# First weight panel, decay groups and squares moved within the opening of a hybrid decoder layer

## The chip, the cores and the metric

One core of a Trainium2 chip runs the whole kernel. The metric is the device time of one execution in microseconds (us). TensorE is PE in the profile (PEld its weight loads), VectorE is DVE, ScalarE is ACT, GpSimd is POOL, and SyncE (SP) issues the transfers.

## The reference, cut to what matters

One inference step of a decoder layer for two request groups that share weights: 1024 prompt tokens and 8 sequences of 4 sample tokens, 1056 tokens of 1024 features. The part that the change touches is the start:

```python
h = rmsnorm(x, norm_mix)                 # x * rsqrt(mean(x*x) + eps) * gain
proj = h @ w_in                          # 1024 -> 3592 columns: q, k, v, a, b, z and the short convolution
log_a = -exp(a_log) * softplus(proj[..., OFF_A:OFF_B] + dt_bias)   # decay of the delta rule, 4 columns
beta = sigmoid(proj[..., OFF_B:OFF_Z])                             # 4 columns
```

Behind it come the convolution and SiLU of q, k and v, the chunked gated delta rule, the short convolution mixer, the output projection, an MLP of 1024 to 4096 to 1024, an embedding gate, and a last norm. All are in float32.

## The kernel before, in words

Every float32 product is made of three products in a faster format: a value is split into a high part (rounded) and a low part (value minus high part), and high by high, low by high and high by low are summed. ACT makes the high parts, DVE and POOL the low ones. Activations lie as features by tokens (`act_hi`, `act_lo`), and the norm's factor per token is not applied to x but to the products, so that the products may start before the sums of squares are known.

The opening works on nine tiles of x, `x_tok[0]` to `x_tok[8]`: eight of 128 tokens and one of the 32 sample tokens. Each tile has two halves of four blocks of 128 features, numbered i = 2t and 2t+1. For a half, PE turns four blocks into one of four PSUM banks `bk[i % 4]` (line 753); DVE multiplies the bank by the norm's gain into one of four SBUF buffers `ring[i % 4]` (line 1575, "weighing"); ACT copies the buffer into `act_hi` (the high part; the helper's line is 1150); and the low part, buffer minus high part, is made by DVE for the even half (line 1578) and by POOL for the odd half (line 2127). PE may reuse a bank once it is weighed (`xw_made`), and DVE may reuse a ring buffer once its low part exists (`xlo_even`, `xlo_odd`). The ring and the banks hold two tiles.

The first weight panel, number 0, holds the eight columns for the decay and beta. ACT splits it (`split_w(0, 0)`, all 1024 columns of elements), and DVE makes its small low part of 64 columns (line 1538, same helper `split_w`). Its products with the tokens are three "decay groups", `ab_group(0)` to `ab_group(2)`, each of 16 matmuls over a third of the tokens (352): `ab_group(0)` needs tiles 0 to 2, `ab_group(1)` needs tiles 0 to 5. DVE copies each result out (`ab_rows`, line 1564) over the place of `x_tok[0]` and the first bytes of `x_tok[1]`, so the first of these waits for the first two sums of squares. Panel 1 is the first of the q columns; `first_group(n)` are its 24 matmuls for third n.

The sums of squares of x by token (`square(t)`, on ACT, 1024 elements a row) lead to the norm's factor: a square root on ACT, a reciprocal, two diagonals `AT` and a small one `X` on DVE (lines 1586 to 1591), and then four matmuls on PE that spread the factor over the partitions (lines 777 to 779), behind `first_group(1)`.

Every engine runs its list strictly in the order written. PE has: turns of tiles 0 to 4, `ab_group(0)`, turns of 5 to 7, `ab_group(1)`, turns of 8, the turns of the old states (lines 764 and 766), `first_group(0)`, `ab_group(2)`, `first_group(1)`, the spreading matmuls, `first_group(2)`, and then the panels one after the other. ACT has: high parts of tile t, then `square(t)` for t up to 3, `split_w(0)` behind tile 2 and `split_w(1)` behind tile 5; behind tile 8 come squares 4 to 8 and the root. DVE has: for each tile its weighing and its low part, `split_w(0)` behind tile 3, `split_w(1)` behind tile 6, `ab_rows(0)` behind tile 5, `ab_rows(1)` and `ab_rows(2)` behind tile 8. SP issues the loads of x and of panel 0 first (line 538 and 526). Its load of panel 2 waits for the split of panel 0, its load of panel 3 for that of panel 1.

Of the kernel before, what the change touches and what calls it, by code (L numbers as in the profile page):

```python
# [18 lines left out]
NTT = TP // P  # L19
# [222 lines left out]
def trunk(nc, x_p, x_s, st_qkv, st_gdn, st_sc, p_p, p_s, norm_mix, w_in, w_cq, a_log, dt_bias, w_gn, w_cs,  # L242
# [19 lines left out]
    with ctx:  # L262
# [127 lines left out]
        sm = Signals(sem)  # L390
# [4 lines left out]
        def at(base, p=0, step=1):  # L395
            return base if isinstance(p, int) and p == 0 else p * step + base

        def twelfths(b, p, q):
            return at(12 * b + q, p, 24)

        def cols(n):
            return slice(n * TH, (n + 1) * TH)

        def tokens(t):
            return P if t < NTT else TS

        def heads(ap):
            return ap.rearrange("p (h t) -> p h t", h=H)

        def spread(ap, n):  # L410

            return ap[:, :, None].to_broadcast([ap.shape[0], ap.shape[1], n])
# [35 lines left out]
        def last_product(hf, g):  # L448

            return (g // 3, g % 3) if hf == 0 else (g % 4, g // 4)  # L450
# [238 lines left out]
        def _(pe):  # L689
            mm, turn = nc.tensor.matmul, nc.tensor.transpose  # L690

            def products(bank, terms):

                for i, (w, a) in enumerate(terms):
                    last = mm(pg[bank][:, 0:TH], w, a, start=i == 0, stop=i == len(terms) - 1)  # L695
                return last
# [7 lines left out]
            def panel_ready(b, p):  # L704
                pe.wait_ge(sm.w_lo_made, at(b + 1, p, 2))
# [10 lines left out]
            def ab_group(n):  # L716

                terms = [(w_hi[0][:, k, :], a[:, k, cols(n)]) for k in range(KD) for a in (act_hi, act_lo)]
                products(n, terms).then_inc(sm.ab_mm, 1)
# [24 lines left out]
            for t in range(NTT + 1):  # L744
                n = tokens(t)
                pe.wait_ge(x_loaded[t], 16)
                for hf in range(2):
                    i = 2 * t + hf
                    if i >= 4:
                        pe.wait_ge(sm.xw_made, i - 3)  # L750
                    for k in range(4):
                        f = slice((4 * hf + k) * P, (4 * hf + k + 1) * P)
                        last = turn(bk[i % 4][:, k * P:k * P + n], x_tok[t][0:n, f], ident[0:n, 0:n])
                    last.then_inc(sm.x_turned, 1)

                if t in (4, 7):
                    whole = 3 if t == 4 else 6
                    pe.wait_ge(sm.xlo_even, whole)
                    pe.wait_ge(sm.xlo_odd, whole)
                    panel_ready(0, 0)  # L760
                    ab_group((t - 4) // 3)
            pe.wait_ge(sm.states_in, 32)
            for j in range(NQ):
                turn(bk[4][:, j * 24:(j + 1) * 24], st_in[:, j * P:(j + 1) * P], ident[0:24, 0:24])
# [373 lines left out]
            for g in range(12):  # L1138
                d, n = last_product(1, g)
# [8 lines left out]
        def _(act):  # L1148
            def op(out, in_, func, **kw):
                return nc.scalar.activation(out, in_, func, **kw)  # L1150

            def split_w(b, p):

                if isinstance(p, int) and b + 2 * p == 2:
                    act.wait_ge(sm.ab_mm, 3)
                elif b >= 2:
                    act.wait_ge(sm.mm_done, twelfths(b - 1, p, 0))
                act.wait_ge(raw_in[b % 2], at(16 * (b // 2 + 1), p, 16))
                act.wait_ge(sm.consts_made, 3)
                op(w_hi[b % 2][:, :, :], w_raw[b % 2][:, :, :], ACT.Copy).then_inc(sm.w_hi_made, 1)  # L1160
# [6 lines left out]
            def square(t):  # L1167

                n = tokens(t)
                if t == 0:  # L1170
                    act.wait_ge(sm.r_tok_set, 2)
                else:
                    act.wait_ge(sm.x_squared, t)
                op(x_sqr[0:n, :], x_tok[t][0:n, :], ACT.Square, accum_out=r_tok[0:n, t:t + 1]) \
                    .then_inc(sm.x_squared, 1)

            act.wait_ge(sm.consts_made, 3)
            for t in range(NTT + 1):
                n = tokens(t)
                for hf in range(2):  # L1180
                    i = 2 * t + hf
                    act.wait_ge(sm.xw_made, i + 1)
                    op(act_hi[:, 4 * hf:4 * hf + 4, t * P:t * P + n], ring[i % 4][:, :, 0:n], ACT.Copy) \
                        .then_inc(sm.xhi_made, 1)
                if t < 4:
                    square(t)
                if t in (2, 5):
                    split_w((t - 2) // 3, 0)
            for t in range(4, NTT + 1):
                square(t)  # L1190
            act.wait_ge(sm.x_squared, NTT + 1)
            op(r_tok[:, :], r_tok[:, :], ACT.Sqrt, scale=1.0 / D, bias=eps[:, 0:1]).then_inc(sm.r_chain, 1)
# [303 lines left out]
            for hf in range(2):  # L1496
# [15 lines left out]
                for g in range(12):  # L1512
                    d, n = last_product(hf, g)
# [16 lines left out]
        def _(dve):  # L1530
            tt, ts_, stt = nc.vector.tensor_tensor, nc.vector.tensor_scalar, nc.vector.scalar_tensor_tensor

            def split_w(b, p):

                dve.wait_ge(sm.w_hi_made, at(b + 1, p, 2))
                if isinstance(p, int) and b + 2 * p == 0:

                    tt(w_hi[0][:, :, 2 * H:AB], w_raw[0][:, :, 0:2 * H], w_hi[0][:, :, 0:2 * H].bitcast(f32), SUB) \
                        .then_inc(sm.w_lo_made, 1)
                    return  # L1540
                tt(w_lo[b % 2][:, :, :], w_raw[b % 2][:, :, :], w_hi[b % 2][:, :, :].bitcast(f32), SUB) \  # L1541
                    .then_inc(sm.w_lo_made, 1)
# [16 lines left out]
            def ab_rows(n):  # L1559

                dve.wait_ge(sm.ab_mm, n + 1)
                if n == 0:
                    dve.wait_ge(sm.x_squared, 2)
                nc.vector.tensor_copy(qkv[0:AB, 0, cols(n)], pg[n][0:AB, 0:TH]).then_inc(sm.ab_kept, 1)


            dve.wait_ge(sm.gain_in, 16)
            for t in range(NTT + 1):
                n = tokens(t)
                for hf in range(2):  # L1570
                    i = 2 * t + hf
                    dve.wait_ge(sm.x_turned, i + 1)
                    if i >= 4:
                        dve.wait_ge(sm.xlo_odd if hf else sm.xlo_even, t - 1)
                    tt(ring[i % 4][:, :, 0:n], heads(bk[i % 4])[:, :, 0:n], spread(n_mix[:, 4 * hf:4 * hf + 4], n), MUL) \
                        .then_inc(sm.xw_made, 1)
                dve.wait_ge(sm.xhi_made, 2 * t + 1)
                tt(act_lo[:, 0:4, t * P:t * P + n], ring[2 * t % 4][:, :, 0:n],
                   act_hi[:, 0:4, t * P:t * P + n].bitcast(f32), SUB).then_inc(sm.xlo_even, 1)
                if t in (3, 6):  # L1580
                    split_w((t - 3) // 3, 0)
                if t in (5, 8):
                    ab_rows((t - 5) // 3)
            ab_rows(2)
            dve.wait_ge(sm.r_chain, 1)
            nc.vector.reciprocal(r_tok[:, :], r_tok[:, :]).then_inc(sm.r_chain, 1)
# [485 lines left out]
            for hf in range(2):  # L2072
# [18 lines left out]
                for g in range(12):  # L2091
                    d, n = last_product(hf, g)
# [288 lines left out]
```

## Time and profile before

| | us |
|---|---|
| median of 3 runs | 1523.75 (1523.41 to 1523.84) |
| the profiled execution | 1522.49 |
| its span | 1520.7 |
| PE busy in the span | 1479.3 |
| DVE busy | 734.0 |
| ACT busy | 474.0 |
| POOL busy | 246.6 |

The profile is of one execution. Its span runs from the first to the last recorded instruction, and its own time is 1.8 us longer than the span. A timeline row gives the start and the duration in us, the engine, the line, the operation, what it writes and reads, and in brackets how long the engine sat idle before it and what released it. A row that ends in x2 or x24 merges so many instructions. Instructions of one engine are pipelined, so a row's duration is somewhat more than its share of the engine's time.

### The profile page before, as it was taken

The numbers are of one execution on the slowest core, as the hardware profiler recorded it, in microseconds if no ns is written. First come the engines' busy times: TensorE is split into PE (matmuls) and PEld (weight loads), VectorE is DVE, ScalarE is ACT, GpSimd is POOL, SyncE is SP. The second block draws the span as 40 slices with busy tenths as digits, with TensorE's granted clock in tenths as the row PEclk, the third lists the DMA queues.
The fourth block names the chain that finished last, engine by engine and source line by source line (L and its number), as shares of the span: only waits on it lengthen the run. The fifth ranks groups of instructions, "written<-read, shape, count | busy, mean of one in ns | idle before, by whom it ended". The sixth has DMA issues, their size and how long they took to land.

```text
span 1520.7 us, 24673 instructions
## 1 busy us (share of the span) xinstructions
PE 1479.3 (97%) x9324; PEld 1449.6 (95%) x9324; DVE 734.0 (48%) x1313; ACT 474.0 (31%) x854; POOL 246.6 (16%) x306
## 2 busy tenths in 40 slices
PE   7999899899999999999999999999999999999997
PEld 6999898699999989999999999999999999998997
DVE  5676943287685553543333333333333334335525
ACT  6323343233243332533122130221203122135525
POOL 3200311143535363100000000000000000041303
PEclk9999998799999999999999999999999999999999
DMA  7112211412122344111111111111111111112102
GB/s 176 49 36 57 76 51 47 133 35 71 29 84 83 87 98 86 42 56 42 42 42 56 42 42 56 42 42 42 56 42 42 56 42 42 56 42 64 35 28 114
DMA packets 166315, 89.83 MB, mean 59 GB/s; under 512 B 50763, under 2 KB 160267, under 8 KB 166230
## 3 DMA queue, kind: packets, MB, share of 16 engines
q1 hardware_dynamic: 165222, 84.89, 20.1%
q0 software_dynamic: 1008, 3.79, 0.6%
q8 instruction: 55, 0.90, 0.3%
q14 instruction: 30, 0.25, 0.1%
HBM read 77.97 MB, written 10.69 MB: 58 GB/s over the span
## 4 chain that ended last, share of the span: by engine, by line
PE 88%; DVE 5%; issue 2%; POOL 2%; ACT 1%; DMA 0%; DVEq 0%; POOLq 0%; SPq 0%
PE pg L695 66%; PE pg L813 12%; PE bk L870 1%; DVE act_lo L1973 1%; PE bk L884 1%; PE bk L888 1%; PE bk L1021 1%; PE bk L840 1%; POOL act_lo L2296 1%; DVE cv L1621 0%; PE bk L854 0%; PE bk L933 0%; PE bk L930 0%; PE bk L938 0%; PE bk L921 0%
## 5 line engine op out<-in xcount | busy, mean ns | idle before, releaser
L695 PE MATMUL pg<-act_hi,w_hi 128*128 128x352 f32 x1344 | 436.1, 325 | 8.0 <-issue 3.6
L695 PE MATMUL pg<-act_lo,w_hi 128*128 128x352 f32 x1344 | 432.3, 322 | 0.0
L695 PE MATMUL pg<-act_hi,w_lo 128*128 128x352 f32 x1320 | 423.7, 321 | 0.0
L695 PEld LDWEIGHTS pg<-act_hi,w_hi 128*128 128x128 f32 x1344 | 253.1, 188 | 11.3 <-issue 7.3
L695 PEld LDWEIGHTS pg<-act_lo,w_hi 128*128 128x128 f32 x1344 | 253.7, 189 | 0.0
L695 PE MATMUL pg<-u_hi,w_hi 128*128 128x352 f32 x768 | 249.3, 325 | 0.0
L695 PE MATMUL pg<-u_hi,w_lo 128*128 128x352 f32 x768 | 248.9, 324 | 0.0
L695 PEld LDWEIGHTS pg<-act_hi,w_lo 128*128 128x128 f32 x1320 | 248.0, 188 | 0.0
L695 PE MATMUL pg<-u_lo,w_hi 128*128 128x352 f32 x768 | 247.8, 323 | 0.0
L1150 ACT ACTIVATE w_hi<-w_raw 128x1024 fp32r<-128x1024 f32 x111 | 117.0, 1054 | 350.4 <-PE pg L695 320.1
L2337 POOL TENSOR_TENSOR ssq<-ssq,sq 128x352 f32<-128x352 f32 x72 | 76.2, 1067 | 875.1 <-ACT sq L1150 874.4
L2034 DVE TENSOR_TENSOR xres<-xres,pg 128x352 f32 (+1 forms) x192 | 99.2, 520 | 201.0 <-PE pg L695 201.0
L1541 DVE TENSOR_TENSOR w_lo<-w_raw,w_hi 128x1024 fp32r<-128x1024 f32 x110 | 139.3, 1266 | 65.4 <-ACT w_hi L1150 65.2
L813 PE MATMUL pg<-act_hi,w_hi 128*128 128x352 f32 x480 | 162.7, 339 | 2.0 <-DVE pre L1598 1.6
L813 PE MATMUL pg<-act_hi,w_lo 128*128 128x352 f32 x480 | 162.3, 338 | 0.0
L813 PE MATMUL pg<-act_lo,w_hi 128*128 128x352 f32 x480 | 160.0, 333 | 0.0
L695 PEld LDWEIGHTS pg<-u_hi,w_hi 128*128 128x128 f32 x768 | 145.0, 189 | 0.0
L695 PEld LDWEIGHTS pg<-u_lo,w_hi 128*128 128x128 f32 x768 | 144.5, 188 | 0.0
L695 PEld LDWEIGHTS pg<-u_hi,w_lo 128*128 128x128 f32 x768 | 143.9, 187 | 0.0
L1150 ACT ACTIVATE sq<-tm 128x352 f32<-128x352 f32 x96 | 47.8, 498 | 231.8 <-DVE tm L2020 231.8
L2024 DVE TENSOR_TENSOR u_lo<-sq,u_hi 128x352 f32 x96 | 50.4, 525 | 129.1 <-ACT u_hi L1150 129.1
L813 PEld LDWEIGHTS pg<-act_hi,w_hi 128*128 128x128 f32 x480 | 93.2, 194 | 7.9 <-issue 5.8
(331 smaller groups left out, 1655.5 us busy)
## 6 DMA issues: line engine op xcount, KB each, us to landing
w_raw<-in_w_up SPq DMA_DIRECT2D x32, 512.0 KB, 4.0
w_raw<-in_w_down SPq DMA_DIRECT2D x32, 512.0 KB, 3.3
w_raw<-in_w_in SPq DMA_DIRECT2D x29, 512.0 KB, 4.4
x_tok<-in_x_prompt SPq DMA_DIRECT2D x8, 512.0 KB, 7.4
w_raw<-in_w_out SPq DMA_DIRECT2D x8, 512.0 KB, 4.1
x_col<-in_x_prompt SPq DMA_DIRECT2D x32, 128.0 KB, 2.6
w_raw<-in_w_ple_gate SPq DMA_DIRECT2D x8, 512.0 KB, 3.9
out<-y_tok SPq DMA_DIRECT2D x8, 512.0 KB, 2.9
```

Source lines behind the costliest of these rows:

```text
L695: last = mm(pg[bank][:, 0:TH], w, a, start=i == 0, stop=i == len(terms) - 1)
L813: last = mm(pg[n][:, 0:TH], w, (act_hi, act_lo, act_hi)[r][:, k, cols(n)], start=k == 0 and r == 0, stop=k == KD - 1 and r == 2)
L840: last = mm(bk[4][:, c:c + 8], S_in[:, h, i, :], F0[:, c:c + 8], start=True, stop=True)
L870: per_head(lambda h, v: mm(A[x][:, v], LY[x][:, h, :], X[x][:, h, :], start=True, stop=True)) \
L884: last = per_head(lambda h, v: mm(A[x][:, v], XT[s][x][:, h, :], LY[x][:, h, :], start=True, stop=True))
L888: last = per_head(lambda h, v: mm(bank[:, v], LY[x][:, h, :], XT[s][x][:, h, :], start=True, stop=True))
L1021: mm(bk[c % 4][:, :], F0[0:TS, c // 2 * P:(c // 2 + 1) * P], by_seq[c % 4][0:TS, :, :], start=True, stop=True).then_inc(sm.q_pe, 1)
L1150: return nc.scalar.activation(out, in_, func, **kw)
L1541: tt(w_lo[b % 2][:, :, :], w_raw[b % 2][:, :, :], w_hi[b % 2][:, :, :].bitcast(f32), SUB) \
L2024: tt(rows(u_lo[c % 2][:, k, cols(n)]), sq[g % 2][:, :], rows(u_hi[c % 2][:, k, cols(n)]).bitcast(f32), SUB).then_inc(sm.u_lo_made, 1)
L2034: tt(x_t, x_t, pg[g % 3][:, 0:TH], ADD).then_inc(sm.evacuated, 2)
L2337: tt(ssq[:, cols(n)], ssq[:, cols(n)], sq[g % 2][:, :], ADD).then_inc(sm.ssq_added, 1)
```

## The change

On PE the first two decay groups go one tile earlier: `ab_group(0)` behind tile 3 and `ab_group(1)` behind tile 6. On ACT, `split_w(0)` goes behind tile 1 (from 2), `split_w(1)` stays behind tile 5, and the squares follow three tiles behind the high parts: `square(t - 3)` from tile 3 on, and squares 5 to 8 after the loop. On DVE the weighing of tile t+1 stands ahead of the low part of tile t, `split_w(0)` goes behind the low part of tile 1 (from 3), `split_w(1)` behind that of tile 5 (from 6), and `ab_rows(0)` and `ab_rows(1)` behind tiles 4 and 7 (from 5 and 8).

```diff
@@ PE
-                if t in (4, 7):
-                    whole = 3 if t == 4 else 6
-                    pe.wait_ge(sm.xlo_even, whole)
-                    pe.wait_ge(sm.xlo_odd, whole)
+                if t in (3, 6):
+                    pe.wait_ge(sm.xlo_even, t)
+                    pe.wait_ge(sm.xlo_odd, t)
                     panel_ready(0, 0)
-                    ab_group((t - 4) // 3)
+                    ab_group((t - 3) // 3)
@@ ACT
-                if t < 4:
-                    square(t)
-                if t in (2, 5):
-                    split_w((t - 2) // 3, 0)
-            for t in range(4, NTT + 1):
+                if t in (1, 5):
+                    split_w((t - 1) // 4, 0)
+                if 3 <= t < NTT:
+                    square(t - 3)
+            for t in range(NTT - 3, NTT + 1):
                 square(t)
@@ DVE
-            for t in range(NTT + 1):
+            def x_weighed(t):
...
+            x_weighed(0)
+            for t in range(NTT + 1):
+                n = tokens(t)
+                if t < NTT:
+                    x_weighed(t + 1)
                 dve.wait_ge(sm.xhi_made, 2 * t + 1)
                 tt(act_lo[:, 0:4, t * P:t * P + n], ring[2 * t % 4][:, :, 0:n],
                    act_hi[:, 0:4, t * P:t * P + n].bitcast(f32), SUB).then_inc(sm.xlo_even, 1)
-                if t in (3, 6):
-                    split_w((t - 3) // 3, 0)
-                if t in (5, 8):
-                    ab_rows((t - 5) // 3)
+                if t in (1, 5):
+                    split_w((t - 1) // 4, 0)
+                if t in (4, 7):
+                    ab_rows((t - 4) // 3)
```

## Rows read from the trace of the kernel before

**Rows 1.** The page: the chain that ended last, by engine.
```profile
PE 88%; DVE 5%; issue 2%; POOL 2%; ACT 1%; DMA 0%; DVEq 0%; POOLq 0%; SPq 0%
```

**Rows 2.** Window: length; PE, PEld, DVE, ACT, POOL busy; granted clock; DMA.
```profile
44.00:130.00 86.00, 86.00 (x547) 85.84 (x547) 59.59 (x98) 23.61 (x40) 7.01 (x35) 1.00 0.13 36
```

**Rows 3.** Timeline of PE where the norm's factor comes in.
```profile
40.88 0.32 PE L695 MATMUL pg<-act_hi,w_lo 128*128 128x352 f32 x1
41.57 1.12 PE L777 MATMUL bk<-AT,ones 128*128 128x512 f32 x2 [0.37 <-DVE X L1591]
```

**Rows 4.** Timeline of ACT: high parts, squares, table load, root.
```profile
23.71 1.23 ACT L1150 ACTIVATE act_hi<-PT 128x512 fp32r<-128x512 f32 x2 [3.76 <-DVE PT L1575]
...
31.26 1.05 ACT L1150 ACTIVATE x_sqr<-x_tok 128x1024 f32<-128x1024 f32 x1
...
37.15 1.28 ACT L1150 ACT_TABLE_LOAD   x1
38.44 0.30 ACT L1150 ACTIVATE r_tok<-r_tok,eps 128x9 f32<-128x9 f32 x1
```

**Rows 5.** Timeline of PE, 7 to 27 us: turns and decay groups.
```profile
7.20 1.97 PE L753 MATMUL bk<-ident,x_tok 128*128 128x128 f32 x8 [0.46 <-DMA x_tok<-in_x_prompt]
...
10.27 5.38 PE L753 MATMUL bk<-ident,x_tok 128*128 128x128 f32 x24 [1.10 <-DMA x_tok<-in_x_prompt]
...
18.23 0.40 PE L695 MATMUL pg<-act_hi,w_hi 128*128 128x352 f32 x1 [2.58 <-DVE w_hi L1538]
...
18.63 0.32 PE L695 MATMUL pg<-act_hi,w_hi 128*128 128x352 f32 x1
...
20.72 0.49 PE L695 MATMUL pg<-act_hi,w_hi 128*128 128x352 f32 x1
...
21.89 3.34 PE L753 MATMUL bk<-ident,x_tok 128*128 128x128 f32 x24
...
26.39 0.40 PE L695 MATMUL pg<-act_hi,w_hi 128*128 128x352 f32 x1 [1.16 <-issue]
```

**Rows 6.** Timeline of DVE: low part, small split, weighing, copy of a decay group.
```profile
12.90 0.69 DVE L1578 TENSOR_TENSOR act_lo<-XT,act_hi 128x512 fp32r<-128x512 f32 x1
...
16.78 1.31 DVE L1538 TENSOR_TENSOR w_hi<-w_raw,w_hi 128x64 fp32r<-128x64 f32 x1
...
24.99 0.51 DVE L1564 COPY qkv<-pg 16x352 f32<-16x352 f32 x1
25.42 1.27 DVE L1575 TENSOR_TENSOR XT<-bk,n_mix 128x512 f32<-128x512 f32 x2
```

**Rows 7.** Timeline of POOL: the odd low parts of tiles 2 and 3.
```profile
13.71 1.29 POOL L2127 TENSOR_TENSOR act_lo<-XT,act_hi 128x512 fp32r<-128x512 f32 x1 [1.04 <-ACT act_hi L1150]
16.73 1.27 POOL L2127 TENSOR_TENSOR act_lo<-PT,act_hi 128x512 fp32r<-128x512 f32 x1 [1.74 <-ACT act_hi L1150]
```

**Rows 8.** The load of panel 0, issued at 2.37 us: KB, us to landing.
```profile
w_raw<-in_w_in SPq DMA_DIRECT2D x1, 512.0 KB, 6.6
```

**Rows 9.** Windows of the turns alone: length, PE busy, granted clock, DMA.
```profile
11.00:15.00 4.00, 4.00 (x20) 1.00 1.03 410
22.00:23.00 1.00, 1.00 (x6) 0.50 1.02 7
23.25:24.75 1.50, 1.50 (x17) 1.00 0.88 199
```

**Rows 10.** Windows of PE: length, busy, granted clock, DMA.
```profile
20.00:21.50 1.50, 1.50 (x7) 0.50 0.68 5
157.00:163.00 6.00, 5.93 (x22) 0.50 0.00 0
298.50:303.00 4.50, 0.00 (x0) 0.99 0.99 282
304.00:309.50 5.50, 5.50 (x22) 0.50 0.21 55
265.50:282.00 16.50, 16.50 (x33) 0.50 0.50 160
```

## The prediction, made before the changed kernel was run

> **What bounds the kernel now.** I read the page first, then busy time by stretch, then the start of the chain of waits, and last the timelines of each engine up to 45 us. The chain that ended last is 88% PE [rows 1], and from 44 to 130 us PE is busy without a gap [rows 2], with what follows hanging on its products. So whatever the opening gains or loses arrives behind it one for one. The opening ends at 41.57 us, where PE starts the matmuls that spread the norm's factor. It waited 0.37 us for DVE's `X`, its last product before ends at about 41.04 (the row at 40.88 is the last of its pace of 0.16), so PE's own list is 0.5 us behind being the bound there [rows 3]. Both must come earlier for a gain; one of them later is enough for a loss.
>
> Two chains, then. ACT's: squares 4 to 8 start at 31.26, follow each other every 1.18 us (five to 37.15), the table load takes 1.28, the root starts at 38.44 [rows 4], and `X` is out at about 41.5, 3.1 later. PE's: turns of tiles 2 to 4 from 10.27 for 5.38; idle for 2.6 until the small split of panel 0; `ab_group(0)` from 18.23; turns of 5 to 7 from 21.89; 1.1 idle; `ab_group(1)` from 26.39 [rows 5]; tile 8, turns of the states and 64 matmuls in a row (24, 16 and 24, 10.3 us).
>
> **The change part by part.** *Panel 0 on DVE and ACT.* Before, the small split ran 16.78 to 18.09, 1.31 for 64 columns [rows 6]. It ended right behind POOL's low part of tile 3, 16.73 to 18.00 [rows 7]: DVE's operations on two SBUF operands and POOL's exclude each other in this trace, while the weighings, which read PSUM, pass. Now ACT splits the panel behind tile 1. The weighing of tile 1 can't start before its turns (7.20 to 9.17, [rows 5]), so its high parts end at about 10.5, the split (1.05 in the page's group) at 11.5; the panel's load, issued at 2.37, lands 6.6 later, at 9.0 [rows 8]. DVE's low part of tile 1 still follows the weighing of tile 2, at 12.90 [rows 6], as tile 2's turns begin at 10.27 when it lands, and the small split goes at 13.5, ahead of POOL's low part of tile 2 at 13.71.
>
> *Start of `ab_group(0)`.* What is late next is the even low part of tile 2. It stands behind the weighing of tile 3: 13.65 to 14.9 (a pair is 1.27, [rows 6]). It then meets POOL's low part of tile 2, 13.71 to 15.00 [rows 7], and runs 15.0 to 15.7. `ab_group(0)` starts at 15.8 instead of 18.23: 2.45 us earlier. Without that exclusion it would be 15.7.
>
> *PE's clock.* The row says 1.00 for the early turns, but 24 turns in 5.38 us are 0.224 each. Where the row says 0.50, they go at that pace (6 met in 1 us), and at a true 1.00 some 0.12 each (17 met in 1.5 us) [rows 5, 9]. So PE starts at the lower level (1.2 GHz) and the profile's row only shows 1.00 for lack of an earlier record. It was at 2.4 GHz by 18.2 (matmuls 0.16 apart), fell at 19.7 behind the idle 2.6 us, and `ab_group(0)` ended at the low pace, 0.29 apart [rows 5, 10]. The Trainium skill says the same of the start ("TensorE: Matmul & The Clock Gate", section "What's actually happening"): the default is the throttled state, and activity releases it; it also warns of idle gaps. By the page's row alone (2.4 GHz from the start) `ab_group(0)` would take 2.6 us and the change would come out as my second case below; by the skill's it starts slow.
> Now PE has done 3.6 us of turns (10.27 to 13.86) and idled 1.9 when `ab_group(0)` starts. The rises in this trace stand behind 5.4 us of turns, 6 us of work (157 to 163) and 5.5 us (304 to 309.5) [rows 5, 10]. Bounds: 16 matmuls at 0.16 are 2.6, at 0.29 are 4.7. I take the level as low for 13 and high for the last 3, 4.3 us, near the low end: the end at 20.1. Behind it come turns of tiles 4 to 6 at 0.12, to 23.1 (before: 5 to 7, to 25.2).
>
> *`ab_group(1)`.* It needs the even low part of tile 5. Before, DVE made low parts while PE was in `ab_group(0)`; now the low part of tile 3 stands behind the weighing of tile 4, whose turns stand behind `ab_group(0)`. From 20.1: first half turned and seen, 0.7; weighing 4, 1.3; low 3, 0.6; weighing 5, 1.25; low 4, 0.6, and 0.3 more against POOL's odd low part of tile 4; `ab_rows(0)`, 0.45; weighing 6, 1.25; low 5, 0.7; PE's start, 0.1 (prices from [rows 6], back to back somewhat under a row's duration). That is 7.2 in all with rounding: 27.1 to 27.3, against 26.39: **+0.75**. DVE becomes the bound here, and PE idles 4.0 us (23.1 to 27.1) where it idled 1.1.
>
> *Clock again.* In 298.5 to 303 the clock fell inside an idle of 5.5 us and PE then worked 5.5 us at 0.50 [rows 10]; at 18 it fell behind one of 2.6. I take it that it falls in the idle of 4.0. Bounds for `ab_group(1)`: nothing, if it doesn't, and 16 x 0.133 = 2.1 if all its matmuls are slow, with slow turns behind. I take 10 slow ones: **+1.3**.
>
> *The tile that moved.* Between `ab_group(1)` and `first_group(0)` PE now turns tile 7 too, 8 x 0.12 = **+0.95**, and a gap of 0.1 before tile 8 goes: **-0.1**. So `first_group(0)` starts at 33.6 instead of 30.7, +2.9, and PE is through `first_group(1)` at 43.95 instead of 41.04. There it no longer waits for `X`: **-0.5**. Sum **+2.4**.
>
> *Squares.* One of five leaves the end of ACT's list, -1.18 in ACT's chain, but tile 8's high part is late: weighing 7 at 31.6, low 6, weighing 8 at 33.5, high part to 34.6, four squares to 39.3, table, root at 40.6, `X` at 43.7. The saving is hidden behind PE (43.95). Square 1, for which `ab_rows(0)` waits, ends at 23.9, before 24.7. The squares 0, 2 and 3 fill idle time of ACT. `split_w(1)` on DVE goes at about 27 with `ab_group(1)` beside it; SP's load of panel 3 moves with it, from 28.6, and its panel is wanted tens of us later. Nothing else is issued more or less often.
>
> The profiled execution had 1522.49 with a span of 1520.7; the sum makes it 1524.9. The runs' median is 1.26 above the profiled one, so **1526.15**, 0.16% above 1523.75. A measurement of this kernel can tell about 0.2% (3 us) from nothing, so in that sense this is no change.
>
> **Rivals.** *Second case: the clock is high by 16 us and stays.* For it: the early rows say 1.00, and tile 3's turns before it are much like those that did release it. Against it: the idle of 4 us is longer than the one that cost the clock. `ab_group(0)` ends at 18.4, DVE's 7.0 puts `ab_group(1)` at 25.4, `first_group(0)` at 30.7, as before; ACT's root is 0.3 earlier and the waiting 0.37 shrinks: -0.35, 1523.4. If the clock is high for the first group and falls before the second, 25.4 start, 9 slow matmuls and slow turns put `first_group(0)` at 32.2: +0.9, 1524.7.
> *Third case, slower: the clock comes back late.* The place is `ab_group(1)` and the turns behind it. If the clock rises only some 6 us into work, as from 157 to 163 and from 304 on [rows 10], all 16 matmuls are slow (+0.8 more) and tile 7's turns (+0.8). The start of `first_group(0)` is then 35.2, the sum +4.0, 1527.8. It decides from an idle of PE long enough for the clock to fall before `ab_group(1)` starts. For it: the two rows. Against: the rise at 23.0 came 4.8 us after work began at 18.2.
> *Fourth case: later falls of the clock meet other work.* There are stretches at 0.50 in which PE is the chain, 265.5 to 282 and 304 to 309.5 [rows 10]. Their work at twice the pace would be 8 and 3 us. If the clock's changes don't move with the work, a shift of 1 to 3 us lengthens or shortens them by a few us. Runs 0.4 us apart speak for a steady pattern that a shift could break. Taken with cases one or two this gives 1520 to 1529.
> *The change doesn't do what it says:* `ab_group(0)` could start no earlier if panel 0 were late; the load's landing at 9.0 excludes it.
>
> **How the numbers follow.** Forecast case 0.45, second case (with its half-way form) 0.27, third 0.13, fourth beyond 3 us either way 0.15, rather more of it fast. The range takes the first three with 1 us around the ends and part of the fourth: 1521.2 to 1528.6; the likeliest case's own is 1525.0 to 1527.3. Slower by over 3 us (above 1526.8): a fifth of the forecast case's upper edge (0.09), the third (0.12) and a part of the fourth: 0.25. Faster by over 3 us (below 1520.7): 0.11, nearly all by the fourth, as no term of the opening gives more than 1 us. Within: 0.64.
>
> **What would show it.** `ab_group(0)` at 15.8 and its matmuls 0.29 apart at first; DVE idle from 15.7 to about 20.8; `ab_group(1)` at 27.1 behind DVE's low part of tile 5, with PE idle 4 us before; `first_group(0)` at 33.6; PE at line 777 at 44.0 with no wait for `X`. The forecast is wrong if line 777 starts before 41.6, if the clock stays high through both groups, or if the traces' difference at 130 us is not that at 44 us.

## The result, and the profile after

The changed kernel takes 1527.53 us in the median of 22 runs (1524.04 to 1529.71), the kernel before 1524.32 in 22 runs beside it (1521.59 to 1526.02): ratio 1.0020, interval 1.0014 to 1.0027, some 3 us slower. A second set (`after_again`, below) gave 1.0013 (1.0004 to 1.0022). The forecast was +2.4 us, 1526.15. Here and below a time is the median of the runs; the ratio is estimated from all of them, with its 95% interval in brackets, and needn't be that of the two medians.

The profiled execution took 1526.67 with a span of 1524.9. The first view is the timeline of PE (start, duration, engine, line, what it writes and reads, in brackets the idle time before and what ended it). It answers to [rows 5] and [rows 3]. A matmul of a group starts 0.16 us behind the one before at the higher clock and 0.29 behind it at the lower.

```profile
10.50 3.45 PE L753 MATMUL bk<-ident,x_tok 128*128 128x128 f32 x16 [1.08 <-DMA x_tok<-in_x_prompt]
...
16.75 0.32 PE L695 MATMUL pg<-act_lo,w_hi 128*128 128x352 f32 x1
...
17.41 0.49 PE L695 MATMUL pg<-act_hi,w_hi 128*128 128x352 f32 x1
...
19.76 3.10 PE L753 MATMUL bk<-ident,x_tok 128*128 128x128 f32 x24
26.87 0.43 PE L695 MATMUL pg<-act_hi,w_hi 128*128 128x352 f32 x1 [4.01 <-DVE act_lo L1584]
...
43.80 0.32 PE L695 MATMUL pg<-act_hi,w_lo 128*128 128x352 f32 x1
44.15 1.12 PE L776 MATMUL bk<-AT,ones 128*128 128x512 f32 x2
```

The second is the chain of waits over the same stretch (start, duration, engine, what it writes, line). It shows when each group began and how long it took, up to the end of its last matmul, which is somewhat behind the start of what follows.

```profile
15.85 4.12 PE pg L695 x16
...
26.87 4.39 PE pg L695 x16
...
33.72 10.40 PE pg L695 x64
```

The reader is to see that the first decay group starts 2.4 us sooner than before (15.85 for 18.23) and the second half a microsecond later (26.87 for 26.39), behind 4.0 us in which PE has nothing to do. From then on everything is late: the first spreading matmul (line 776) starts at 44.15 instead of 41.57, +2.58. In the first group the quick matmuls come first (16.75) and the slow ones behind (17.41).

Third, DVE's timeline (columns as above). Between the low part at 15.11 and the weighing at 20.72 it stands idle for 4.9 us, and then the low parts of tiles 3 (21.92), 4 and 5 stand in a row, each behind the weighing of a later tile. The last row is the making of `X`.

```profile
13.72 0.22 DVE L1537 TENSOR_TENSOR w_hi<-w_raw,w_hi 128x64 fp32r<-128x64 f32 x1
...
15.11 0.68 DVE L1584 TENSOR_TENSOR act_lo<-XT,act_hi 128x512 fp32r<-128x512 f32 x1
20.72 1.29 DVE L1575 TENSOR_TENSOR XT<-bk,n_mix 128x512 f32<-128x512 f32 x2 [4.93 <-PE bk L753]
21.92 0.68 DVE L1584 TENSOR_TENSOR act_lo<-PT,act_hi 128x512 fp32r<-128x512 f32 x1
22.71 1.29 DVE L1575 TENSOR_TENSOR PT<-bk,n_mix 128x512 f32<-128x512 f32 x2
23.91 0.68 DVE L1584 TENSOR_TENSOR act_lo<-XT,act_hi 128x512 fp32r<-128x512 f32 x1
...
24.95 1.27 DVE L1575 TENSOR_TENSOR XT<-bk,n_mix 128x512 f32<-128x512 f32 x2
26.14 0.67 DVE L1584 TENSOR_TENSOR act_lo<-PT,act_hi 128x512 fp32r<-128x512 f32 x1
...
42.83 1.26 DVE L1597 TENSOR_SCALAR X<-ident,r_tok 32x32 f32<-32x32 f32 x1
```

Fourth, windows of PE (length, busy, granted clock, DMA share, GB/s). The clock is at the lower level (0.50 is 1.2 GHz) for most of both groups. In both it was still at the higher level when the group started (the matmuls up to 16.91 are 0.16 us apart, and the row at 27.00 has 1.00) and fell at 17.0 and at 27.3. From 44 to 130 us PE is busy all the time, as in [rows 2], so most of the 2.6 us is carried on: the matmuls of line 813 (812 in the changed kernel) begin at 129.64 before and at 132.01 now, +2.4.

```profile
17.00:18.00 1.00, 1.00 (x6) 0.50 1.15 186
...
27.00:27.20 0.20, 0.20 (x2) 1.00 0.57 4
27.50:30.50 3.00, 3.00 (x12) 0.50 0.65 24
...
44.00:130.00 86.00, 85.97 (x541) 1.00 0.14 38
```

The spans differ by 4.2 us, and the remaining 1.6 us comes later: the row at 304.00 in [rows 10]'s stretch, where PE resumes behind a wait of 5.5 us, answers to one at 308.09, +4.1. How much of that is the change is asked below.

### The profile page after: what moved, and what is told of

Same layout as the page of the kernel before. It is cut to its first block, busy times and chain, and to the rows that moved or that the text cites. A ratio compares the mean times of both kernels' runs of the same rounds, so it can differ in the third digit from the quotient of the medians.

```text
span 1524.9 us, 24673 instructions
## 1 busy us (share of the span) xinstructions
PE 1480.6 (97%) x9324; PEld 1451.0 (95%) x9324; DVE 733.2 (48%) x1313; ACT 473.9 (31%) x854; POOL 245.8 (16%) x306
## 4 chain that ended last, share of the span: by engine, by line
PE 89%; DVE 5%; issue 2%; POOL 2%; ACT 1%; DMA 0%; SPq 0%; DVEq 0%; POOLq 0%
PE pg L695 67%; PE pg L812 12%; PE bk L869 1%; DVE act_lo L1979 1%; PE bk L883 1%; PE bk L887 1%; PE bk L1020 1%; PE bk L839 1%; POOL act_lo L2302 1%; PE bk L1130 1%; DMA x_tok<-in_x_prompt 0%; DVE cv L1627 0%; PE bk L853 0%; PE bk L932 0%; PE bk L929 0%
```

## The experiments

The theory is that of the prediction: the first decay group stands ahead of tile 4's turns, so DVE has nothing to do during it and pays its low parts afterwards; PE waits for them, the clock falls in or just behind the wait, and a tile's turns are left for behind the second group. The rivals: weighing a tile ahead is the fault; both groups' places count alike; the squares set the end; or it is the clock's chance. All ratios are to the kernel before, run on the same chip.

**Both groups back** (`groups_back`).

```diff
-                if t in (3, 6):
+                if t in (4, 7):
...
-                if t in (4, 7):
-                    ab_rows((t - 4) // 3)
+                if t in (5, 8):
+                    ab_rows((t - 5) // 3)
```

> The changed kernel with only its decay groups back behind tiles 4 and 7 (their copies on DVE behind tiles 5 and 8). Theory: the loss comes from PE standing behind a decay group while DVE's low part of an older tile stands behind a weighing that PE hasn't turned yet, and from the clock that falls in that idle. With tile 4 turned before the first group, DVE has work during it: first group at 15.9 us, second at about 23.2 (26.87 in the changed kernel), first_group(0) at 27.6, first spreading matmul at about 38 (44.15), so about 6 us faster than the changed kernel and 3.5 us faster than the kernel before. Rival, that weighing a tile ahead is what costs: second group still at 26 or later and the spreading matmul above 42, no gain over the kernel before.

Measured: 1520.48 against 1524.35, 0.9974 (0.9965 to 0.9984), 3.9 us faster than before. The timeline and the chain of this kernel:

```profile
15.89 0.43 PE L695 MATMUL pg<-act_hi,w_hi 128*128 128x352 f32 x1 [0.24 <-DVE act_lo L1584]
...
23.13 0.43 PE L695 MATMUL pg<-act_hi,w_hi 128*128 128x352 f32 x1 [1.79 <-DVE act_lo L1584]
...
37.80 1.02 PE L776 MATMUL bk<-AT,ones 128*128 128x512 f32 x2
```

```profile
15.89 2.84 PE pg L695 x16
...
23.13 2.84 PE pg L695 x16
```

All of the forecast starts are met within 0.2 us, and both groups take 2.84 us instead of 4.12 and 4.39. Everything else of the change, weighing ahead included, is still in this kernel. So the loss lies in where the groups stand.

**DVE's order back** (`low_first`).

```diff
-            x_weighed(0)
             for t in range(NTT + 1):
                 n = tokens(t)
-                if t < NTT:
-                    x_weighed(t + 1)
+                x_weighed(t)
```

> The changed kernel with only DVE's order back (weighing of a tile directly ahead of its own low part). Theory: the low part of tile 3 leaves the chain to the second group and that of tile 4 is done sooner, but PE still turns tile 4 behind the first group: second group at about 26.0 us (26.87), first_group(0) at 32.9, spreading matmul at 43.4, about 0.7 us faster than the changed kernel and 1.9 slower than before. Rival, that weighing ahead is the whole loss: spreading matmul at 41.6 or earlier, no slower than the kernel before.

Measured: 1528.84 (6 runs) against 1524.35, 1.0029 (1.0017 to 1.0041). The second group started at 26.08 for the 26.0 forecast, but that is luck: the forecast went by a slow first group, and here the first was fast (2.81 us). Where it was fast with the new order (`after_again`), the second started at 25.40, so the old order makes it 0.7 us later, not 0.9 sooner (one profile each). The clock was low through all of the second group and the spreading matmul came at 44.15, not at 43.4:

```profile
26.08 5.03 PE pg L695 x16
...
44.15 1.12 PE bk L776 x2
```

The forecast time was missed by 2.6 us (4.5 slower than before for 1.9 forecast). What follows is that the order isn't the fault: with the old order the changed kernel is no better.

**The early split alone** (`split_alone`), in the kernel before.

```diff
+                if t == 1:
+                    split_w(0, 0)
                 if t < 4:
                     square(t)
-                if t in (2, 5):
-                    split_w((t - 2) // 3, 0)
+                if t == 5:
+                    split_w(1, 0)
...
-                if t in (3, 6):
-                    split_w((t - 3) // 3, 0)
+                if t in (2, 6):
+                    split_w((t - 2) // 4, 0)
```

> The kernel before with only the split of panel 0 early (ACT behind the high parts of tile 1, DVE behind the low part of tile 2). Theory: the first group starts at about 15.7 us (18.23) right behind the turns of tile 4, PE doesn't idle, the clock stays at the higher level, the second group starts at about 22.4, first_group(0) at 26.5, spreading matmul at about 37: some 4 us faster than before. Rival, that an early split gains nothing since ACT's squares set the spreading matmul: it stays at 41.5, same time as before.

Measured: 1521.96 against 1524.35, 0.9981 (0.9973 to 0.9990), 2.4 us faster. The spreading matmul came at 38.31, later than the 37 forecast, and PE waited for `X`:

```profile
38.31 1.12 PE L777 MATMUL bk<-AT,ones 128*128 128x512 f32 x2 [0.37 <-DVE X L1593]
```

This part of the change is worth 3.3 us in the opening. The rival (that it stays at 41.5) falls, since tile 8 and with it the last five squares also come sooner (the first of them at 28.01 instead of 31.26).

**Work for PE in the wait** (`filler`), in the changed kernel.

```diff
+                if t == 6:
+                    for r in range(22):
+                        mm(pg[2][:, 0:TH], w_hi[0][:, r % KD, :], act_hi[:, r % KD, cols(0)], start=True, stop=True)
```

> The changed kernel with 22 more matmuls of 352 columns on PE between the turns of tile 6 and the second decay group, written to a bank that nothing reads before it is written anew; they fill about 3.5 of the 4 us of idle time. Theory: the clock stays at the higher level in the second group, which takes 2.6 instead of 4.4 us; the spreading matmul comes at about 42.5 (44.15), 1.6 us faster than the changed kernel, about 1 slower than before. Rival, that the clock isn't part of the loss: second group as long as before, or the filler delays it, 0 to 0.5 us slower than the changed kernel.

Measured: 1524.34 against 1524.35, 1.0000 (0.9992 to 1.0009): with 22 needless matmuls the changed kernel is as fast as the kernel before. Its chain:

```profile
15.41 5.06 PE pg L695 x16
...
27.51 2.83 PE pg L695 x16
...
43.25 1.13 PE bk L779 x2
```

The second group took 2.83 us instead of 4.39. The first was slow throughout in this execution (5.06 for 4.12), which is why the spreading matmul came at 43.25 and not at 42.5. That the clock is part of the loss is shown by this kernel; the runs put that part at 2 to 3 us, the trace at 1.5, and the difference between these is not settled.

**One group back at a time** (`first_back`, `second_back`), in the changed kernel.

```diff
-                if t in (3, 6):
+                if t in (4, 6):
...
-                if t in (4, 7):
-                    ab_rows((t - 4) // 3)
+                if t in (5, 7):
+                    ab_rows((t - 5) // 2)
```

> The changed kernel with only its first decay group back behind tile 4 (the second stays behind tile 6; DVE copies behind tiles 5 and 7). Theory: the first group's place is what costs, since tile 4's weighing then runs beside it: first group at 15.9 us, second at 23.1, tile 7 is turned behind it, first_group(0) at 28.5, spreading matmul at about 38.8: 5 us faster than the changed kernel, 1 us slower than with both groups back. Rival, that both places count alike: second group at 25 or later, spreading matmul at 41.

```diff
-                if t in (3, 6):
+                if t in (3, 7):
...
-                if t in (4, 7):
-                    ab_rows((t - 4) // 3)
+                if t in (4, 8):
+                    ab_rows((t - 4) // 4)
```

> The changed kernel with only its second decay group back behind tile 7 (the first stays behind tile 3; copies behind tiles 4 and 8). Theory: the second group still starts at 26.9 us, as DVE's low part of tile 5 is what it waits for; tile 7's turns move into the idle time, so first_group(0) comes 0.95 sooner, at 32.8, spreading matmul at 43.2, 1 us faster than the changed kernel and 1.6 slower than before; more if the shorter idle time keeps the clock. Rival, that both places count alike: second group at 25, spreading matmul at 41.

`first_back`: 1522.61 against 1524.08, 0.9983 (0.9974 to 0.9992). `second_back`: 1524.96 against 1524.08, 1.0007 (0.9998 to 1.0016). Chains of the first and of the second:

```profile
15.89 2.83 PE pg L695 x16
...
23.13 4.36 PE pg L695 x16
...
40.39 0.86 PE bk L777 x2
```

```profile
15.28 2.84 PE pg L695 x16
...
24.75 5.06 PE pg L695 x16
...
45.30 0.86 PE bk L777 x2
```

Moving the first group back brings the second to 23.13 as forecast. Behind the idle of 2.7 us that then stands before it the clock still fell, at 24.0 (4.36 us for the group), so the spreading matmul came 1.5 us later than forecast. With only the second back, the second group waits as DVE's list says: 24.75, 2 us sooner than forecast, because the first group ran fast here (2.84). But the clock fell at 24 and stayed low to 38, and the profile is that of one of the slowest of its 11 runs. By the medians against the kernel before, the first group's place costs 3.6 to 4.8 us and the second's 1.2 to 2.4, and the two add up to the 6 to 7 us between `groups_back` and the changed kernel. The rival that they count alike falls.

**The squares** (`squares_alone`, `split_squares`), in the kernel before, without and with the early split of `split_alone`.

```diff
-                if t < 4:
+                if t < 5:
                     square(t)
...
+                if t == 6:
+                    square(5)
-            for t in range(4, NTT + 1):
+            for t in range(6, NTT + 1):
```

> The kernel before with squares 4 and 5 moved from the end of ACT's list to behind the high parts of tiles 4 and 6, and nothing else. Theory: X is 2 us sooner, but PE's own list ends at 41.04 us, so the spreading matmul moves from 41.57 to 41.1, and the time by less than the runs can tell (0 to 0.5 us faster). Rival, that ACT's squares were the bound: spreading matmul at 39.5, 2 us faster.

> The kernel before with the early split of panel 0 and with squares 4 and 5 moved from the end of ACT's list to behind the high parts of tiles 4 and 6. Theory: with the split alone PE waited 0.4 us for X at 38.3; two squares fewer at the end put the root 2 us sooner, PE's list is the bound, spreading matmul at 37.9, 0.4 us faster than the split alone. Rival, that the squares delay the high parts of tiles 5 and 7: second group above 23.5 us and spreading matmul above 38.3.

`squares_alone`: 1521.79 against 1523.66, 0.9993 (0.9984 to 1.0002); its spreading matmul at 40.71, with no wait for `X`: PE's own list was the bound, and the rival's 39.5 was not reached. Its turns ran fast from 10 us on, and part of the 0.9 us against before may be chance. The runs show no difference beyond their interval, which reaches from 2.4 us faster to 0.3 slower; a gain of up to 2 us isn't excluded by them. `split_squares`: 1518.56 (only 5 runs) against 1524.08, 0.9962 (0.9948 to 0.9976); its chain has the matmul directly behind PE's own list, as forecast:

```profile
23.20 2.81 PE pg L695 x16
...
27.61 10.40 PE pg L695 x64
38.00 0.86 PE bk L777 x2
```

Run once more:

> The kernel before with the early split of panel 0 and squares 4 and 5 moved up, once more, since its first median rests on 5 runs. Theory: the opening is worth 3.7 us (spreading matmul at 37.8 instead of 41.57) and the rest of the first median, 1518.56 against 1524.08, was chance: ratio 0.9975, 3.7 us faster. Rival, that it is worth 5.5 us: ratio 0.9962 again.

1521.87 (11 runs) against 1523.84, 0.9985 (0.9976 to 0.9994): 2 us faster, less than either forecast had. The spreading matmul was at 37.67 in this one, as worked out. Both sets together put it some 2 to 5.5 us below the kernel before; it can't be told from `groups_back` by these. All three, `groups_back`, `best` and this one, beat the kernel before and the changed one.

**Second group behind all turns** (`best`), in the changed kernel. The squares also come two tiles behind the high parts instead of three.

```diff
-                if t in (3, 6):
+                if t == 4:
...
             last.then_inc(sm.st_turned, 1)
+            pe.wait_ge(sm.xlo_even, 6)
+            pe.wait_ge(sm.xlo_odd, 6)
+            ab_group(1)
             panel_ready(U_QKV, 0)
...
+                if t == 3:
+                    square(0)
                 if 3 <= t < NTT:
-                    square(t - 3)
-            for t in range(NTT - 3, NTT + 1):
+                    square(t - 2)
+            for t in range(NTT - 2, NTT + 1):
...
-                if t in (4, 7):
-                    ab_rows((t - 4) // 3)
+                if t in (5, 8):
+                    ab_rows((t - 5) // 3)
```

> The changed kernel with its first decay group back behind tile 4, its second behind the turns of tile 8 and of the states, so that these fill PE's wait for the low part of tile 5, and squares two tiles behind. Theory: PE hardly idles from 10.5 us on: second group at 23.2, first_group(0) at 25.9, spreading matmul at 36.2, 1.6 us faster than with both groups back at 7, 5.4 faster than the kernel before. Rival, that DVE and ACT (root at 32.7, X at 35.8 at best) or the split of panel 1 set the end: first_group(0) waits, spreading matmul at 37 to 38.

Measured: 1520.26 against 1524.08, 0.9972 (0.9963 to 0.9981), 3.8 us faster than before, 1.6 less than forecast and no better than `groups_back`. Its spreading matmul came 3 us later than forecast (39.28 for 36.2). The clock fell in the first group (4.38 us for 2.84), behind an idle of 1.5 us, and again behind the small turns. In its chain 80 matmuls follow each other without a wait, and yet they take 14.5 us:

```profile
15.15 4.38 PE pg L695 x16
...
24.76 14.52 PE pg L695 x80
39.28 0.86 PE bk L779 x2
```

```profile
22.00:23.00 1.00, 0.32 (x5) 1.00 1.15 8
23.00:24.00 1.00, 0.90 (x15) 1.00 0.75 84
...
25.00:26.00 1.00, 1.00 (x8) 0.99 1.28 181
26.00:27.00 1.00, 1.00 (x5) 0.50 0.64 5
```

Filling a wait with small turns did not keep the clock in this execution: it fell at 26, with PE nearly always busy since 23. Before it fell PE had waited 0.7 us (from 22.2), made small turns for 1.9 us, and then matmuls of 352 columns for 1.3 us.

**The same kernels again** (`before_again`, `after_again`, no edit).

> The kernel before once more, to see how much two executions of one kernel differ. Theory: the clock's changes don't keep their place against the work from one execution to the next, so the changes in the opening lie at other times than 19.7 and 23.0 us and the first spreading matmul moves by up to 1 us around 41.6, and the end by up to 3 us; ratio to the kernel before 1.000 within 0.001. Rival, that the clock changes at the same times in each execution: 19.7 and 23.0 again within 0.2 us.

> The changed kernel once more. Theory: the first group at 15.5 to 15.9 us and the second behind DVE's low part of tile 5 again, with PE idle 3 to 5 us before it, but the number of slow matmuls in each group differs; spreading matmul between 42.5 and 45; ratio to the kernel before 1.002. Rival, that the first profile was a lucky or an unlucky one: spreading matmul below 42.5.

`before_again`: 1524.22 against 1523.66, 1.0003 (0.9994 to 1.0012). `after_again`: 1525.79, 1.0013. Windows of PE in the kernel before, first as profiled for this, then again; below them those of the changed kernel again:

```profile
17.25:19.25 2.00, 1.02 (x6) 1.00 1.22 229
20.75:22.75 2.00, 2.00 (x10) 0.50 0.90 6
```

```profile
17.25:19.25 2.00, 0.90 (x3) 0.50 1.21 210
20.75:22.75 2.00, 2.00 (x8) 0.50 0.51 4
```

```profile
17.25:19.25 2.00, 2.00 (x16) 1.00 1.18 202
...
24.50:26.50 2.00, 1.10 (x4) 0.50 1.21 264
```

The same program is at 2.4 GHz at 18 us in one execution and at 1.2 GHz in the other, so the rival (the clock changes at the same times) falls. The spreading matmul came at 42.73 in `before_again` (41.57 in the first) and at 43.77 in `after_again` (44.15). PE resumes at 304.00 and 305.28 in the two executions of before, at 308.09 and 306.77 in those of the changed kernel. So the two kernels differ there by 1.5 to 4.1 us, by which executions one takes, and what the first profiles gained behind 130 us may be chance: from the start of line 813 (812) to that row the two executions of before take 174.4 and 174.5 us, those of the changed kernel 176.1 and 174.9.

## Why the prediction was right

The time came out, and so did most of its terms; the clock in the first group was forecast wrongly, and the sum didn't show it.

*Start of `ab_group(0)`.* Forecast 15.8, found 15.85. The small split took 0.22 instead of 1.31, as POOL's low part of tile 2 began behind it, at 13.95. DVE's low part of tile 2 ended at 15.8.

*Clock in the first group.* Forecast: low for 13 matmuls, high for the last 3, the end at 20.1. Found: the other way round, and the sign "its matmuls 0.29 apart at first" didn't come. The clock was at the higher level when the group started and for 1.1 us more (matmuls 0.16 us apart up to 16.91), fell at 17.0, and stayed low for the other nine and into the turns behind, to about 20.4. So this step was wrong as a mechanism: the first group didn't start slow, and the second case's premise (clock high by 16 us) held, though the clock was then lost inside the group, as in the kernel before at 19.7. That the turns behind it started at 19.76, near 20.1, is luck: nine or ten slow matmuls for 13. Over the kernels with this group behind tile 3 it took 4.12 us, 5.06 (`filler`, the only one that started slow) and three times 2.8 (`low_first`, `second_back`, `after_again`).

On the start level the Trainium skill was followed ("TensorE: Matmul & The Clock Gate", section "What's actually happening"), and the traces agree: in every profile here the first eight turns took 1.94 us, the slow pace, beside a row that says 1.00. What was wrong is the step from there to 15.8 us. When the clock first rose differed: by 10 us in `best` and `squares_alone` (8 turns in 1.1 us), by 15.9 in the changed kernel, and in `filler` only behind its first group.

*Second group.* Forecast 27.1, found 26.87, released by DVE's `act_lo` as worked out. The 0.3 us for POOL's low part of tile 4 didn't occur: DVE's low part at 23.91 took 0.68, as POOL's had begun at 22.75 and was all but done. Idle time: forecast 4.0, found 4.01.

*Clock in the second group.* Forecast +1.3 for 10 slow matmuls. From the group's start to the turns behind it there are 4.23 us, 2.75 before, so +1.5. The clock fell at 27.3, just behind the idle and not in it; in `after_again` and `low_first` it fell in it, and all 16 were slow. `filler` shows that this part goes when PE has work in the wait.

*The tile that moved.* Forecast `first_group(0)` at 33.6, found 33.72.

*The squares.* `X` was forecast at 43.7; the root came at 41.02 (40.6 forecast) and `X` ended at 44.09. PE's last product started at 43.80 and the spreading matmul 0.35 behind it, where `groups_back` has 0.15 (37.65 and 37.80). So PE still waited some 0.2 us for `X`, against the forecast of no wait, and the saving of one square shows nowhere, as said.

*The sum.* Forecast +0.75, +1.3, +0.95, -0.1 and -0.5; found +0.48 (start of the second group), +1.48 (its clock), +0.97 (tile 7 and the gap, forecast +0.85) and -0.34 (the wait for `X`). Together +2.4 forecast, +2.58 found at the spreading matmul, +2.4 at 130 us, +2.1 and +3.2 in the two sets of runs. The terms from the second group's clock on came out by the mechanism. Its start came near by luck, since it hangs on the first group's length: with a first group that is fast throughout it is 1.5 us sooner (25.40 in `after_again`). What the sum left out is the later part, which the fourth rival named: the clock's falls meet other work in each execution. Two executions of one kernel differ by 1.3 us at 304 us (1.2 of it already at the spreading matmul), so the median of three runs (1523.41 to 1523.84) looked steadier than the kernel is: 22 runs spread over 4.4 us. The rival's argument "runs 0.4 us apart speak for a steady pattern" was wrong. That the clock stays high through both groups was seen in neither of the changed kernel's two profiles.

The second rival's half-way form (high in the first group, low in the second) is what `after_again` shows: the second group at 25.40, as priced (25.4), but with all 16 matmuls slow for 9, so `first_group(0)` at 33.3 for 32.2 and the spreading matmul +2.2 for +0.9. The third rival (clock back late in the second group) is in the same profile, and in `low_first` and `second_back` at 5.03 and 5.06 us for the group. So the +2.4 was met by two different paths of the clock, and the forecast named only one of them.

## What to carry to other kernels

When a group of matmuls is moved ahead of the work that feeds another engine, ask what that engine will do meanwhile: here DVE idled 4.9 us during the group and PE 4.0 us after it, and the group's own gain of 2.4 us at its start was lost before the next one. Let the feeding steps run first, and put the group where its inputs are ready without a wait, so that one idle stretch doesn't make two. A change that moves a wait of PE should be judged on ten or more runs and by a marker in the timeline, since the clock's chance is as large as such a change.

## What the runs showed of the hardware

The changes of the granted clock don't keep their place against the work: 19.7 and 23.0 us in one execution of the kernel before, 17 and 24 in the next.

The length of an idle stretch of PE doesn't tell by itself whether the clock falls. It fell in the group behind 1.5 us (`best`, first group), 1.9 (the changed kernel, first group) and 2.7 (`first_back`), and stayed high behind 1.7 (`after_again`), 1.8 (`groups_back`) and 1.9 (`low_first`). Behind the longer ones before a decay group (2.2 to 4.8 us) it fell in every profile here, or had fallen before they ended. In six of these cases the group began at the higher level and lost it 0.4 to 1.5 us in. In `best` it fell while PE was busy, behind small turns.

A granted clock of 1.00 ahead of the first recorded change isn't to be relied on: in `filler` the row says 1.00 from the start on, and the first group's matmuls are 0.29 us apart (16 in 5.06 us).

DVE's operations on two SBUF operands wait for POOL's: the 64-column split took 0.22 us alone (at 13.72 in the changed kernel) and 1.31 beside POOL's low part (at 16.78 in the kernel before), and both ended within 0.1 us.
